# Transposing the expert activations: a scratch round trip and VectorE block turns in place of TensorE transposes

## The chip, the cores and the metric

The program runs on 1 core of a Trainium2 chip. The metric is device time in microseconds (us): the span of the core from its first to its last instruction and what lies around it. Lower is better.

## What is computed

A one-layer decoder trunk on 2048 tokens of width 1024, in float32: LayerNorm, a mixer (a projection, pooling and a gated convolution, an output projection), LayerNorm, and a mixture of experts, LayerNorm. The change touches the last part only, whose core is

```python
# each token goes to 2 of 16 experts; rows are sorted by expert and padded to blocks of 128
def expert_block(args):
    xb, e = args                                   # xb (128, 1024)
    hid = jax.nn.silu(xb @ w1[e]) * (xb @ w3[e])   # w1, w3 (1024, 512)
    return hid @ w2[e]                             # w2 (512, 1024)

ybuf = lax.map(expert_block, (xbuf.reshape(n_blocks, EXPERT_BLOCK, d), blk_e))
```

## The kernel before

**Three products for one.** Every float32 operand is split into a high part (`_hi`, a cast to float32r on ScalarE) and the rest (`_lo`, a subtraction on VectorE). `three` (lines 520 to 522) makes a product of three matmuls: high by high, low by high, high by low.

**Blocks and turns.** In these inputs there are 40 blocks, numbered 0 to 39. TensorE (PE in the profile) goes through one turn for each. In turn b it computes `xb @ w1` of block b (24 matmuls, `up(e_of, 0)`), `xb @ w3` (24, `up(e_of, 1)`), transposes the gathered rows of block b+1 (`x_tile`, 8 transposes of 128x128, line 560), computes `hid @ w2` of block b-1 (24, `down`), and transposes the activations of block b (`hid_tile(b)`, 4 transposes into the PSUM bank `aux`, line 830). The blocks 0, 1 and 39 are partly written out by hand; blocks 2 to 38 are a loop.

**The other engines in turn b**, each in the order of its program:

- ScalarE (ACT): four words of the block table (`value_load`), `hid_hi(b-1)` (copies `aux` to `ht_hi`, line 1106), `silu(b)` after the first 24 matmuls (line 1113), if block b is its expert's last the casts of the next expert's two `w1` units (line 921, 1.9 us each), `final_scale`, `gate_col`, `x_hi(b+1)`, if b is an expert's last the two casts of `w3`, and, after `down` has ended and if block b-1 was its expert's last, the two casts of `w2`.
- VectorE (DVE): three table words, `hid_lo(b-1)` (`ht_lo`, line 1586), the two subtractions of `w1` units if b is an expert's last (line 1649, 2.2 us each), `hid_rows(b)` (`hid`, line 1580), `x_lo(b+1)` (`xt_lo`, line 1570), the two subtractions of `w3`, then, after `down(b-1)`, `final_sums` and `final_rows` of block b-1, and the two subtractions of `w2` if block b-1 was its expert's last.
- GpSimd (POOL): index copies, the gather of `xg` for a later block (line 1953), the put and the gather of running sums, `orow` (line 1929, one add over 128x1024), the store of finished rows.
- SyncE issues the 1 MB loads of weight units, one expert ahead, each when the subtraction of the same unit of the expert before is done.

Units of a weight lie in one place only (`ring_hi`, `ring_lo`), so the next expert's `w1` is split between the end of the first 24 matmuls of an expert's last block and the start of the next turn. This text calls a turn in which block b is its expert's last a **switch turn**. Where an expert has two blocks, the turn ahead of its switch turn is the one after the last switch, and the split of its own `w2` ends in the switch turn itself: a **two-block switch turn**. There are six of these, and eight **three-block switch turns**, which have a turn more in between.

Of the kernel before, what the change touches and what calls it, by code (L numbers as in the profile page):

```python
# [29 lines left out]
ALU = mybir.AluOpType  # L30
# [33 lines left out]
ROW = D + NE  # L64
ALIGN = 128
# [29 lines left out]
def build(nc, x, ln_in_g, ln_in_b, w_in, pool_w, pool_scale, conv_w, conv_b, w_out, ln1_g, ln1_b,  # L95
# [15 lines left out]
    w2_v = exp_w2[0].rearrange("(g i) (k p) n -> i g p k n", p=P, g=NEG)  # L111

    with ExitStack() as ctx:
# [174 lines left out]
        hid = e("hid", [P, DE])  # L288
        ht_hi = e("ht_hi", [P, FT, P], F32R)
# [132 lines left out]
        s_htr = sem("hid_transposed")  # L422
        s_hthi = sem("hid_t_hi")
# [34 lines left out]
        def _(sp):  # L458
# [32 lines left out]
            def load_expert(ex, j):  # L491
                v = (w1_v, w3_v, w2_v)[j // 2]
                kts = v.shape[3] // 2
                src = v[ex // NEG, ex % NEG, :, (j % 2) * kts:(j % 2 + 1) * kts, :]
                dst = staged(j)[:, 0, :].rearrange("p (k c) -> p k c", k=kts)
                sp.dma_start(dst, src).then_inc(s_stage[j], 16)
# [20 lines left out]
        def _(pe):  # L517
# [359 lines left out]
            pe.wait_ge(s_plist, 1)  # L877
            hid_tile(1)
# [5 lines left out]
            with pe.Fori(2, nb1) as b:  # L884
# [11 lines left out]
                hid_tile(b)  # L896
# [16 lines left out]
        def _(act):  # L913
# [4 lines left out]
            def split_hi_expert(ex, j):  # L918

                act.wait_ge(s_stage[j], (ex + 1) * 16 + (MU // 2 * 32 if j < 2 else 0))  # L920
                nc.scalar.copy(ring_hi[:, j:j + 1, :], staged(j)).then_inc(s_ehi[j // 2], 1)  # L921
# [180 lines left out]

            def hid_hi(b):
                act.wait_ge(s_htr, b + 1)
                bank = hid_0[:] if isinstance(b, int) and b == 0 else aux[:].rearrange("p (k t) -> p k t", t=P)
                nc.scalar.copy(ht_hi[:], bank).then_inc(s_hthi, 1)
# [20 lines left out]
            def turn(b, first):  # L1127

                e_of = act.value_load(table[0:1, 0, bass.ds(b, 1)], min_val=0, max_val=NE - 1)
                e_next = act.value_load(table[0:1, 0, bass.ds(b + 1, 1)], min_val=0, max_val=NE - 1)  # L1130
                ends = act.value_load(table[0:1, 1, bass.ds(b, 1)], min_val=0, max_val=1)
# [27 lines left out]
            for t in range(TPC):  # L1159
                act.wait_ge(s_ahout[t], 16 * NCH)  # L1160
            silu(0)
# [10 lines left out]
            ended = act.value_load(table[0:1, 1, bass.ds(nb1 - 1, 1)], min_val=0, max_val=1)  # L1172
            hid_hi(nb1 - 1)
            silu(nb1)
            nb2 = act.value_load(nblocks[0:1, 2:3], min_val=NE - 1, max_val=NB - 2)
            final_scale(nb2)
            act.wait_ge(s_htr, nb)
# [9 lines left out]
        def _(dve):  # L1187
# [197 lines left out]
            def route_hots(c, last=False):  # L1385
# [19 lines left out]
                for k in range(2):  # L1405
                    if last and k == 1:
# [4 lines left out]
                        hid_rows(0)  # L1411
# [161 lines left out]
            def hid_rows(b):  # L1573
                dve.wait_ge(s_silu, b + 1)
                dve.wait_ge(s_w3, b + 1)
                if not (isinstance(b, int) and b == 0):
                    dve.wait_ge(s_htr, b)
                dve.wait_ge(s_gcol, b + 1)
                col = gate_0 if isinstance(b, int) and b == 0 else gate[:, bass.ds(b, 1)]
                V.scalar_tensor_tensor(out=hid[:], in0=act_a[:], scalar=col, in1=acc[1][:], op0=ALU.mult,  # L1580
                                       op1=ALU.mult).then_inc(s_hid, 1)
# [50 lines left out]
            ch.mark(V.tensor_copy(table[:, 1, :], f_next[:]))  # L1632
# [81 lines left out]
            def turn(b, first, split=True):  # L1714
                e_of = dve.value_load(table[0:1, 0, bass.ds(b, 1)], min_val=0, max_val=NE - 1)
                ends = dve.value_load(table[0:1, 1, bass.ds(b, 1)], min_val=0, max_val=1)
# [13 lines left out]
                if first:  # L1730
                    hid_lo(b)
# [316 lines left out]
```

## Time and profile before

| | us |
|---|---|
| median of 3 runs | 1350.07 (1349.74 to 1353.28) |
| span of the profiled execution | 1348.3 |
| its first 634 us | mixer and routing, untouched by the change |
| turns of blocks 2 to 39 | from about 651 to 1328 |
| PE busy | 1311.4 (97% of the span) |
| DVE, ACT, POOL busy | 958.4, 511.7, 525.1 |

Only the span of the profiled execution is known, not a time of its own; the median lies 1.8 us above it. Times of rows are counted from the start of the span. A matmul of 128x512 is listed with some 390 ns, but a new one starts every 0.227 us, since they overlap.

### The profile page before, as it was taken

To read this page: it belongs to the slowest core of one execution; us is meant where nothing else is said; L and a number is where in the kernel's file an instruction comes from. 1 tells how busy PE (TensorE), PEld (TensorE's weight loads), DVE (VectorE), ACT (ScalarE), POOL (GpSimd) and SP (SyncE) were. 2 spreads that over 40 slices of the span, in tenths; PEclk is the share of its full clock that TensorE was granted. 3 is DMA by queue.
4 is the path that set the end of the run, shared out by engine and by line. 5 is a ranking of instruction groups with operands and counts; after the bars stand their busy time and mean duration, and the time that the engine had idled before them with its cause. 6 is when DMAs were issued, how large, how long until landed. Compare 5 with 4: busy or idle time off the path is not lost. (4 is left out here: it accounts for less than half of the span.)

```text
span 1348.3 us, 20368 instructions
## 1 busy us (share of the span) xinstructions
PE 1311.4 (97%) x6382; PEld 1095.8 (81%) x6383; DVE 958.4 (71%) x1357; ACT 511.7 (38%) x568; POOL 525.1 (39%) x543
## 2 busy tenths in 40 slices
PE   5999999999999999998999999999999999999995
PEld 5888888888888888887888888888888888888884
DVE  7758577687759785698777886665675677776564
ACT  3423234322443234323444454343443454434241
POOL 2001010111101110022566665755665656666555
PEclk9999999999999999999999999999999999999998
DMA  9625434563455344544777774563554545666421
GB/s 266 181 89 162 149 111 163 170 192 109 156 186 158 110 141 159 208 181 169 287 263 256 271 270 147 193 234 132 181 202 181 191 164 214 236 231 238 142 69 64
DMA packets 156522, 243.58 MB, mean 181 GB/s; under 512 B 18944, under 2 KB 84992, under 8 KB 156480
## 3 DMA queue, kind: packets, MB, share of 16 engines
q1 hardware_dynamic: 118624, 154.15, 35.3%
q0 software_dynamic: 28928, 71.74, 15.0%
q10 hardware_dynamic: 8928, 17.13, 3.7%
q8 instruction: 26, 0.43, 0.1%
q14 instruction: 16, 0.13, 0.0%
HBM read 211.97 MB, written 64.62 MB: 205 GB/s over the span
## 5 line engine op out<-in xcount | busy, mean ns | idle before, releaser
L520 PE MATMUL acc<-ring_hi 128*128 128x512 f32 (+1 forms) x800 | 308.8, 386 | 2.1 <-DVE ring_lo L1239 1.9
L522 PE MATMUL acc<-ring_hi,ring_lo 128*128 128x512 f32 (+1 forms) x800 | 305.6, 382 | 0.0
L521 PE MATMUL acc<-ring_lo,ring_hi 128*128 128x512 f32 (+1 forms) x800 | 305.3, 382 | 0.0
L520 PE MATMUL acc<-ring_hi,xt_hi 128*128 128x512 f32 x648 | 256.7, 396 | 4.1 <-issue 2.8
L522 PE MATMUL acc<-ring_hi,xt_lo 128*128 128x512 f32 x648 | 252.8, 390 | 0.0
L521 PE MATMUL acc<-ring_lo,xt_hi 128*128 128x512 f32 x648 | 252.4, 390 | 0.0
L1802 POOL TENSOR_TENSOR small<-small 128x1 f32<-128x1 f32 x31 | 47.4, 1527 | 360.8 <-DVE small L1208 360.8
L520 PEld LDWEIGHTS acc<-ring_hi 128*128 128x128 f32 x800 | 151.3, 189 | 30.1 <-DVE ring_lo L1239 2.5
L522 PEld LDWEIGHTS acc<-ring_hi,ring_lo 128*128 128x128 f32 x800 | 151.2, 189 | 29.1
L521 PEld LDWEIGHTS acc<-ring_lo,ring_hi 128*128 128x128 f32 x800 | 151.3, 189 | 27.7
L921 ACT CAST ring_hi<-stage_x 128x2048 fp32r<-128x2048 f32 x64 | 119.4, 1915 | 76.3 <-PE acc L522 75.8
L520 PEld LDWEIGHTS acc<-ring_hi,xt_hi 128*128 128x128 f32 x648 | 121.8, 188 | 30.3 <-issue 5.9
L522 PEld LDWEIGHTS acc<-ring_hi,xt_lo 128*128 128x128 f32 x648 | 121.6, 188 | 25.8
L521 PEld LDWEIGHTS acc<-ring_lo,xt_hi 128*128 128x128 f32 x648 | 121.8, 188 | 23.9
L1649 DVE TENSOR_TENSOR ring_lo<-stage_x,ring_hi 128x2048 fp32r<-128x2048 f32 x60 | 136.7, 2318 | 0.2
L916 ACT CAST ring_hi<-stage 128x2048 fp32r<-128x2048 f32 x47 | 89.7, 1908 | 103.5 <-PE acc L522 97.3
L1929 POOL TENSOR_TENSOR orow<-arow,b 128x1024 f32<-128x1024 f32 x39 | 106.5, 2731 | 48.6 <-ACT arow L1120 48.6
L520 PE MATMUL acc<-ring_hi,ht_hi 128*128 128x512 f32 x312 | 125.3, 401 | 0.0
L1194 DVE TENSOR_TENSOR ring_lo<-stage,ring_hi 128x2048 fp32r<-128x2048 f32 x47 | 107.6, 2289 | 21.1 <-ACT ring_hi L916 21.0
L522 PE MATMUL acc<-ring_hi,ht_lo 128*128 128x512 f32 x312 | 122.0, 391 | 0.0
L521 PE MATMUL acc<-ring_lo,ht_hi 128*128 128x512 f32 x312 | 121.5, 389 | 0.0
L1661 DVE TENSOR_TENSOR rrow<-srow,acc 128x512 f32<-128x512 f32 x78 | 49.9, 680 | 95.1 <-PE acc L522 95.1
(276 smaller groups left out, 1884.0 us busy)
## 6 DMA issues: line engine op xcount, KB each, us to landing
stage_x<-in_exp_w SPq DMA_DIRECT2D x64, 1024.0 KB, 6.2
stage<-in_w_in SPq DMA_DIRECT2D x64, 512.0 KB, 5.4
stage<-in_exp_w SPq DMA_DIRECT2D x32, 1024.0 KB, 6.6
stage<-in_w_out SPq DMA_DIRECT2D x32, 512.0 KB, 5.3
h_scratch<-hres POOLq DMA_DIRECT2D x16, 512.0 KB, 3.0
sum_scratch<-hres ACTq DMA_DIRECT2D x16, 512.0 KB, 2.9
hrow<-in_x POOLq DMA_DIRECT2D x12, 512.0 KB, 4.8
h_scratch<-hrow POOLq DMA_DIRECT2D x12, 512.0 KB, 3.0
```

The lines of the kernel that those rows point to most:

```text
L520: nc.tensor.matmul(dst, w_hi, x_hi, start=start, stop=False)
L521: nc.tensor.matmul(dst, w_hi, x_lo, start=False, stop=False)
L522: return nc.tensor.matmul(dst, w_lo, x_hi, start=False, stop=stop)
L916: nc.scalar.copy(ring_hi[:, slot:slot + 1, :], staged(slot_in)).then_inc(s_hi, 1)
L921: nc.scalar.copy(ring_hi[:, j:j + 1, :], staged(j)).then_inc(s_ehi[j // 2], 1)
L1194: V.tensor_tensor(lo, staged(slot_in), hi.bitcast(F32), ALU.subtract).then_inc(s_lo, 1)
L1649: V.tensor_tensor(ring_lo[:, j:j + 1, :], staged(j), ring_hi[:, j:j + 1, :].bitcast(F32), ALU.subtract).then_inc(s_elo[w], 1)
L1661: ins = V.tensor_tensor(rrow[:, cols], srow[:, cols], acc[2 + n][:], ALU.add)
L1802: G.tensor_tensor(rstd[:], vareps[:], half[:], ALU.pow).then_inc(s_rstd, 1)
L1929: G.tensor_tensor(orow[:], arow[:], b_2[:], ALU.add).then_inc(s_fo, 1)
```

## The change

The activations of a block no longer go through TensorE. ScalarE stores `hid` (256 KB) in a scratch tensor in HBM, and reads it back with four DMAs of 64 KB, one for each group of 32 partitions, so that partition group a holds columns 128a to 128a+127 of all rows (`hid_q`). One VectorE instruction then transposes all 32x32 blocks of `hid_q` into `aux`. The rows of `w2` are loaded in the matching order, with four DMAs a unit in place of one. Blocks 0 and 39 still use the TensorE transposes; there `hid_rows` writes its columns in that order with four instructions in place of one. The high and low parts of `ht` follow as before, though on ScalarE `silu(b)` now comes ahead of `hid_hi(b-1)`. Row 1 of the block table holds one packed word a block (expert, is it the last of its expert, was the block before), so ScalarE and VectorE read one word a turn.

```diff
-    w2_v = exp_w2[0].rearrange("(g i) (k p) n -> i g p k n", p=P, g=NEG)
+    w2_v = exp_w2[0].rearrange("(g i) (a k c) n -> i g a c k n", a=QUARTERS, c=SUB, g=NEG)
+    hid_dram = nc.dram_tensor("hid_scratch", (P, DE), F32).ap()
+    hid_quarters = hid_dram.rearrange("(b r) (a f) -> a r b f", r=SUB, a=QUARTERS)
...
+                    for a in range(QUARTERS):
+                        src = w2_v[ex // NEG, ex % NEG, a, :, (j % 2) * 2:(j % 2 + 1) * 2, :]
+                        dst = staged(j)[a * SUB:(a + 1) * SUB, 0, :].rearrange("p (k c) -> p k c", k=2)
+                        sp.dma_start(dst, src).then_inc(s_stage[j], 16)
...
                 down(pe_of)
-                hid_tile(b)
...
+            def hid_out(b):
+                act.wait_ge(s_hid, b + 1)
+                act.wait_ge(s_hq, b * 16 * QUARTERS)
+                act.dma_start(hid_dram, hid[:]).then_inc(s_hst, 16)
+
+            def hid_back(b):
+                act.wait_ge(s_hst, b * 16 + 16)
+                for a in range(QUARTERS):
+                    act.dma_start(hid_q[a * SUB:(a + 1) * SUB, :].rearrange("r (b f) -> r b f", f=P), hid_quarters[a])\
+                        .then_inc(s_hq, 16)
...
+                word = act.value_load(table[0:1, 1, bass.ds(b, 1)], min_val=0, max_val=4 * NE - 1)
...
                 if not first:
-                    ended = act.value_load(table[0:1, 1, bass.ds(b - 1, 1)], min_val=0, max_val=1)
+                    silu(b)
                     hid_hi(b - 1)
-                    silu(b)
...
                 x_hi(b + 1)
+                hid_out(b)
                 with act.If(ends > 0):
...
                     units_hi(e_of + 1, 1)
+                hid_back(b)
...
+            def hid_turn(b):
+                dve.wait_ge(s_hq, b * 16 * QUARTERS)
+                V.transpose(aux[:].rearrange("p (k b c) -> p k b c", k=FT, c=SUB),
+                            hid_q[:].rearrange("p (b k c) -> p k b c", k=FT, c=SUB)).then_inc(s_hturn, 1)
...
+                word = dve.value_load(table[0:1, 1, bass.ds(b, 1)], min_val=0, max_val=4 * NE - 1)
...
                 if not first:
-                    ended = dve.value_load(table[0:1, 1, bass.ds(b - 1, 1)], min_val=0, max_val=1)
-                    if split:
-                        hid_lo(b - 1)
+                    hid_turn(b)
+                    hid_lo(b - 1)
```

How the order of the instructions moves is seen best at two places. On ScalarE, in the loop over the blocks, from the copy of `aux` to the casts of `w1` (`ring_hi<-stage`), before:

```order
L1133 TENSOR_LOAD table_221
L1133 ISA x2
L1106 CAST ht_hi_209<-aux 128x512 [waits hid_transposed]
L1113 ACTIVATE act_a_207<-acc0 128x512 [waits hid_rows,w1_used]
L1136 COMPARE_AND_BRANCH
L920 ISA
L921 CAST ring_hi<-stage 128x2048 [waits stage0_in]
L921 CAST ring_hi<-stage 128x2048 [waits stage1_in]
```

The same place in the changed kernel (`hid_quarters_turned` is raised by the new VectorE instruction):

```order
L1157 TENSOR_LOAD table_222
L1157 ISA x2
L1137 REGISTER_ALU
L1141 ACTIVATE act_a_207<-acc0 128x512 [waits hid_rows,w1_used]
L1134 CAST ht_hi_210<-aux 128x512 [waits hid_quarters_turned]
L1163 REGISTER_ALU
L1163 COMPARE_AND_BRANCH
L932 ISA
L933 CAST ring_hi<-stage 128x2048 [waits stage0_in]
L933 CAST ring_hi<-stage 128x2048 [waits stage1_in]
```

The copy to `ht_hi` now stands between the silu and the casts of `w1`, and waits for VectorE. On VectorE, from the end of one turn (the `w2` subtractions) to the `w1` subtractions of the next, in the changed kernel:

```order
L1699 TENSOR_TENSOR ring_lo<-stage_x_226,ring_hi 128x2048 [waits w2_hi]
L1782 UNCONDITIONAL_BRANCH
...
L1627 STREAM_TRANSPOSE aux<-hid_q_209 128x512 [waits hid_quarters_in]
L1633 TENSOR_TENSOR ht_lo_211<-aux,ht_hi_210 128x512 [waits hid_t_hi]
L1771 REGISTER_ALU
L1771 COMPARE_AND_BRANCH
L1698 ISA
L1699 TENSOR_TENSOR ring_lo<-stage,ring_hi 128x2048 [waits w1_hi]
```

Before, `ht_lo` followed the `w2` subtractions with nothing between; now the block transpose of `hid_q` comes first, and `ht_lo` needs the ScalarE copy of what it wrote. Later in the turn, ScalarE has the store of `hid` (waits `hid_rows`) between `x_hi` and the casts of `w3`, which before followed each other:

```order
L1109 CAST xt_hi_205<-tp1 128x512 [waits x_transposed]
L1118 ISA [waits hid_rows]
L1119 DMA hid_scratch<-hid_208 128x512 [waits hid_quarters_in]
L1177 COMPARE_AND_BRANCH
L932 ISA
L933 CAST ring_hi<-stage_x_226 128x2048 [waits stage2_in]
```

So the casts of `w3` have come to stand behind the VectorE instruction that writes `hid`.

## Rows read from the trace of the kernel before

**Rows 1.** The page: busy time of the engines and their shares of the span.

```profile
PE 1311.4 (97%) x6382; PEld 1095.8 (81%) x6383; DVE 958.4 (71%) x1357; ACT 511.7 (38%) x568; POOL 525.1 (39%) x543
```

**Rows 2.** Waits of PE: who waited for whom, total us, times, longest.

```profile
PE acc L520 <- DVE xt_lo L1570: 1.3, 4, 0.4
```

**Rows 3.** PE in order of time: start us, us, what [idle before].

```profile
722.75 0.49 PE L520 MATMUL acc<-ring_hi,xt_hi 128*128 128x512 f32 x1 [0.19 <-issue]
...
911.99 1.04 PE L560 MATMUL tp<-ident,xg 128*128 128x128 f32 x8
912.92 0.49 PE L520 MATMUL acc<-ring_hi,ht_hi 128*128 128x512 f32 x1
...
918.01 0.39 PE L521 MATMUL acc<-ring_lo,ht_hi 128*128 128x512 f32 x1
918.24 0.40 PE L522 MATMUL acc<-ring_hi,ht_lo 128*128 128x512 f32 x1
...
918.83 0.48 PE L520 MATMUL acc<-ring_hi,xt_hi 128*128 128x512 f32 x1
919.15 0.39 PE L521 MATMUL acc<-ring_lo,xt_hi 128*128 128x512 f32 x1
```

**Rows 4.** The tile hid: the PE transposes of it, their count and durations.

```profile
L830 PE MATMUL aux<-ident,hid x156: 270/272/273, 649.4 to 1323.3; 128*128 128x128 f32 x156
```

**Rows 5.** ScalarE in order of time, in a two-block switch turn.

```profile
710.35 0.60 ACT L1113 ACTIVATE act_a<-acc 128x512 f32<-128x512 f32 x1 [1.51 <-PE acc L522]
710.84 3.71 ACT L921 CAST ring_hi<-stage 128x2048 fp32r<-128x2048 f32 x2
```

**Rows 6.** VectorE in order of time, in the same turn.

```profile
708.89 4.49 DVE L1649 TENSOR_TENSOR ring_lo<-stage_x,ring_hi 128x2048 fp32r<-128x2048 f32 x2
713.30 0.68 DVE L1586 TENSOR_TENSOR ht_lo<-aux,ht_hi 128x512 fp32r<-128x512 f32 x1
713.90 6.69 DVE L1649 TENSOR_TENSOR ring_lo<-stage,ring_hi 128x2048 fp32r<-128x2048 f32 x2
...
721.17 1.28 DVE L1570 TENSOR_TENSOR xt_lo<-tp,xt_hi 128x512 fp32r<-128x512 f32 x2
```

**Rows 7.** GpSimd in order of time, in the same turn and the next.

```profile
715.69 2.75 POOL L1929 TENSOR_TENSOR orow<-arow,b 128x1024 f32<-128x1024 f32 x1 [2.27 <-ACT arow L1120]
...
722.92 2.65 POOL L1953 DMA_INDIRECT xg<-h_scratch,gat_now  x1 [0.87 <-POOL gat_now L1943]
```

**Rows 8.** ScalarE: silus of three turns, and two copies that wait for the gather.

```profile
889.01 0.60 ACT L1113 ACTIVATE act_a<-acc 128x512 f32<-128x512 f32 x1 [2.42 <-PE acc L522]
...
911.91 0.19 ACT L1101 COPY gate<-xg  x1 [3.34 <-DMA xg<-h_scratch,gat_now]
...
924.59 0.60 ACT L1113 ACTIVATE act_a<-acc 128x512 f32<-128x512 f32 x1 [1.49 <-PE acc L522]
...
942.28 0.60 ACT L1113 ACTIVATE act_a<-acc 128x512 f32<-128x512 f32 x1 [2.42 <-PE acc L522]
...
1123.28 0.19 ACT L1101 COPY gate<-xg  x1 [2.18 <-DMA xg<-h_scratch,gat_now]
```

**Rows 9.** VectorE in the three-block switch turn of the silu at 889.01.

```profile
891.44 4.49 DVE L1649 TENSOR_TENSOR ring_lo<-stage,ring_hi 128x2048 fp32r<-128x2048 f32 x2 [1.41 <-ACT ring_hi L921]
...
897.82 4.75 DVE L1649 TENSOR_TENSOR ring_lo<-stage_x,ring_hi 128x2048 fp32r<-128x2048 f32 x2
```

**Rows 10.** GpSimd: the gather of rows issued after that turn.

```profile
903.86 1.04 POOL L1953 DMA_INDIRECT xg<-h_scratch,gat_now  x1 [0.89 <-DVE rrow L1661]
```

**Rows 11.** DMA issues: what, queue, count, KB each, median us from issue to landing.

```profile
sum_scratch<-hres ACTq DMA_DIRECT2D x16, 512.0 KB, 2.9
...
xg<-h_scratch,gat_now POOLq DMA_INDIRECT x39, 4.4
...
h1t<-in_pool_w ACTq DMA_DIRECT2D x1, 256.0 KB, 6.6
```

**Rows 12.** ScalarE in order of time: what a DMA issue takes of its sequencer.

```profile
614.57 0.33 ACTq L975 DMA_DIRECT2D sum_scratch<-hres  x1
```

More of the change, by code:

```diff
@@ L288, in build @@
         hid = e("hid", [P, DE])
+        hid_q = e("hid_q", [P, DE])
         ht_hi = e("ht_hi", [P, FT, P], F32R)
@@ L1571, in x_lo, with hid_rows @@
                                     ALU.subtract).then_inc(s_xtlo, 1)
-            def hid_rows(b):
+            def hid_rows(b, by_tile=False):
                 dve.wait_ge(s_silu, b + 1)
                 dve.wait_ge(s_w3, b + 1)
-                if not (isinstance(b, int) and b == 0):
-                    dve.wait_ge(s_htr, b)
+                if isinstance(b, int) and b == 1:
+                    dve.wait_ge(s_htr, 1)
+                elif not (isinstance(b, int) and b == 0):
+                    dve.wait_ge(s_hst, b * 16)
                 dve.wait_ge(s_gcol, b + 1)
                 col = gate_0 if isinstance(b, int) and b == 0 else gate[:, bass.ds(b, 1)]
-                V.scalar_tensor_tensor(out=hid[:], in0=act_a[:], scalar=col, in1=acc[1][:], op0=ALU.mult,
-                                       op1=ALU.mult).then_inc(s_hid, 1)
+                if by_tile:
+                    tiles = hid[:].rearrange("p (k a c) -> p a k c", k=FT, c=SUB)
+                    parts = [(tiles[:, a], *(t[:, a * P:(a + 1) * P].rearrange("p (k c) -> p k c", c=SUB)
+                                             for t in (act_a, acc[1]))) for a in range(QUARTERS)]
+                else:
+                    parts = [(hid[:], act_a[:], acc[1][:])]
+                for to, x_a, x_b in parts:
+                    ins = V.scalar_tensor_tensor(out=to, in0=x_a, scalar=col, in1=x_b, op0=ALU.mult, op1=ALU.mult)
+                ins.then_inc(s_hid, 1)
+            def hid_turn(b):
+                dve.wait_ge(s_hq, b * 16 * QUARTERS)
+                V.transpose(aux[:].rearrange("p (k b c) -> p k b c", k=FT, c=SUB),
+                            hid_q[:].rearrange("p (b k c) -> p k b c", k=FT, c=SUB)).then_inc(s_hturn, 1)
             def hid_lo(b):
@@ L1712, in final_last, with turn @@
                                        op0=ALU.mult, op1=ALU.add).then_inc(s_fo, 1)
-            def turn(b, first, split=True):
-                e_of = dve.value_load(table[0:1, 0, bass.ds(b, 1)], min_val=0, max_val=NE - 1)
-                ends = dve.value_load(table[0:1, 1, bass.ds(b, 1)], min_val=0, max_val=1)
+            def turn(b, first):
+                word = dve.value_load(table[0:1, 1, bass.ds(b, 1)], min_val=0, max_val=4 * NE - 1)
+                e_of, ends, ended = (word >> 2).with_bounds(min_val=0, max_val=NE - 1), word & 2, word & 1
                 if not first:
-                    ended = dve.value_load(table[0:1, 1, bass.ds(b - 1, 1)], min_val=0, max_val=1)
-                    if split:
-                        hid_lo(b - 1)
+                    hid_turn(b)
+                    hid_lo(b - 1)
                 with dve.If(ends > 0):
@@ L1738, in turn_last @@
             def turn_last(b, prev):
[L1739 removed]
+                ended = dve.value_load(table[0:1, 1, bass.ds(b, 1)], min_val=0, max_val=4 * NE - 1) & 1
+                hid_turn(b)
                 hid_lo(b - 1)
[L1741 removed]
+                hid_rows(b, True)
                 dve.wait_ge(s_hthi, b + 1)
@@ L1750, in _ @@
             dve.wait_ge(s_elo[2], 2)
+            dve.sem_inc(s_hturn, 1)
             turn(1, True)
             nb1 = dve.value_load(nblocks[0:1, 1:2], min_val=NE, max_val=NB - 1)
-            turn(2, False, split=False)
-            with dve.Fori(3, nb1) as b:
+            with dve.Fori(2, nb1) as b:
                 turn(b, False)
```

49 lines of the change are left out of this document (28 added, 21 removed).

## The prediction, made before the changed kernel ran

> **What bounds the kernel now.** First the page: PE is busy 97% of the span, every other engine 71% or less [rows 1]. Then the waits of PE: in all the turns it loses only 1.3 us to VectorE's `xt_lo`, in four waits [rows 2]. So the time is the sum of what PE issues, and taking work off PE is worth its full price, as long as nobody else comes late. Then the timelines of one turn, engine by engine, since the question is who has little room. A turn is counted here from PE's first matmul of it; its silu stands 5.76 us in (918.83 [rows 3], 924.59 [rows 8]). An undisturbed turn lasts 942.28 - 924.59 = 17.69 us [rows 8]. A two-block switch turn lasts longer: silu at 710.35 [rows 5], so it begins at 704.59, and the next begins at 722.75 [rows 3]: 18.16 us, since `xt_lo` comes late. VectorE has no room in these turns.
>
> **The transposes taken off PE.** Two matmuls in a row start 0.23 us apart (918.01, 918.24), but from 918.24 to the second matmul after the four transposes, 919.15, it is 0.91 us [rows 3]: they cost 0.91 - 2 x 0.23 = 0.45 us. There are 156 / 4 = 39 such groups [rows 4], and the one of block 39 stays: 38 x 0.45 = **17.3 us less**. An undisturbed turn becomes 17.24 us. The low bound of the gain is what the loop's branch might take by itself once no short transposes stand there: a 0.19 us gap was seen at a turn's start [rows 3], which would leave 10 us of the 17.
>
> **The table words.** ScalarE's and VectorE's table reads stand where these engines wait for PE anyway (ScalarE's silu waits for PE in every turn) or run under the subtractions ahead of them. I cost them at nothing. Not below nothing either: PE would gain only if it waited for them, and it waits 1.3 us in all [rows 2].
>
> **The round trip through scratch.** No row shows this store and this load. The nearest: a 512 KB store of ScalarE lands after 2.9 us, a 256 KB load of 512 B pieces after 6.6 us [rows 11], and an issue takes ScalarE 0.33 us [rows 12]. So from `hid` to `hid_q` it takes 2.9 + 4 x 0.33 + 4.4 to 6.6 = 9 to 11 us. `hid` is written some 12 us into the turn (VectorE's `hid_rows` waits for PE's 48 matmuls), so it is back at 21 to 23, that is 4 to 6 us into the next turn. `ht_lo` is needed when `down` starts, 912.92 against a start at 900.95: 12.0 us in [rows 3, 8]. In undisturbed turns the round trip is hidden, and I cost it at nothing. The DMA page of the Trainium skill (DMA: Bandwidth & Descriptors, the rule on batching) says that transfers under 64 KB are descriptor-dominated; four of 64 KB lie at that edge, and it would matter only if the cover were gone.
>
> **The VectorE transpose** is not in the trace either. Its nearest row is `ht_lo`, 0.6 us from start to start for 128x512 (713.30 to 713.90 [rows 6]); the upper bound is one pass of four times the size, 2.2 us [rows 9]. I take 0.6.
>
> **Two-block switch turns.** Here the added chain is in the open. Before, ScalarE cast `w1` from 710.84 [rows 5], 6.25 us in, long ahead of VectorE. Now these casts stand behind the copy to `ht_hi`, that behind the block transpose, and that behind the two `w2` subtractions. Step by step, us into the turn: the `w2` subtractions began at 708.89 - 704.59 = 4.3 [rows 6], now at 4.7, as the turn begins sooner after `down` ends; two take 4.4, to 9.1; block transpose 0.6, to 9.7; copy 0.6, to 10.3; first cast 1.9 (half of 3.71 [rows 5]), to 12.2; two `w1` subtractions 4.4, to 16.6; `hid` 0.65 and the first `xt_lo` 0.6, to 17.85; PE starts the next turn 0.98 us after the second `xt_lo` begins (721.77 to 722.75 [rows 3, 6]): 18.8 us. That is 1.6 us over 17.24, where before it was 0.47 over 17.69: 1.1 more, six times: **6.7 us more**. One delay disappears in this: before, the two `w1` subtractions took 6.69 instead of 4.4 us [rows 6], because `orow` (from 715.69 [rows 7]) held the second one up. With `arow` 4 us later, `orow` comes to start at 15.1, when the second subtraction (14.4 to 16.6) is already running.
>
> **The gather of the next rows.** `x_tile` needs `xg`, and POOL issues that gather behind `orow` and the subtractions of `w3`. In the trace: `w3` subtractions from 897.82 to 902.5 [rows 9], gather at 903.86 [rows 10], data there at 911.91 (ScalarE waited for it [rows 8]), `x_tile` at 911.99 [rows 3], just in time. Another such turn had it at 1123.28, 1.2 us earlier in the turn [rows 8]. So the slack is 0.1 to 1.2 us.
> Three-block switch turn, changed: the casts of `w3` now wait for `hid` and a DMA issue, and `hid` comes 0.5 later since `ht_hi` is copied ahead of the `w1` casts. The first `w3` subtraction, before 897.82 - 883.25 = 14.6 us in, moves to about 16.2, its pair ends at 20.6, the gather goes out at 22.0, which is 4.8 us into the next turn where it was 2.9. 1.9 later, less the slack, is 0.7 to 1.8 us of waiting of PE; none if POOL's short copies slip in between the two subtractions. I take 0.8, eight times: **6.4 us more**.
> After a two-block switch turn: `orow` ends at 16.6 + 2.4 = 19.0; gather 4.5 us behind its end as before (718.4 to 722.92 [rows 7]) or 5.6 as in the other turn, so 4.7 to 5.8 us into the next turn, and later still if it waits for the `w3` subtractions, which end 5.4 into it. With a landing of 4.4 (the median [rows 11]) to 8.0 us (903.86 to 911.9) it is there between 9.1 and 14, needed at 11.0: 0 to 3 us. `ht_lo` alone costs 0.3 there (start 11.2, usable 12.1, wanted 11.9). I take 1.7, six times: **10.2 us more**.
> The Trainium skill (SBUF — State Buffer, "Who interferes with whom") says that a VectorE instruction with two SBUF inputs and a GpSimd instruction that reads SBUF exclude each other, first come first served. The trace agrees: 6.69 us for the pair of subtractions beside `orow`.
>
> **Start and end.** Two added table instructions and two times four `hid_rows` pieces in place of one: **0.8 us more**.
>
> **The sum.** 1350.07 - 17.3 + 6.7 + 6.4 + 10.2 + 0.8 = **1356.9 us**; on the profiled execution 1348.3 + 6.8 = 1355.1 of span. The differences are taken from that execution and put on the median, 1.8 us above its span. What a measurement of this kernel can tell from no change is 0.3%, 4 us: under 1346.0 is faster, over 1354.1 slower.
>
> **Rivals.**
> 1. *The gathers keep their time*: POOL's copies slip between the subtractions and `xg` lands in 4.4 us. Then only `ht_lo`'s 0.3 x 6 and the switch turns are left: 1350.07 - 17.3 + 6.7 + 1.8 + 0.8 = 1342 us, faster. For it: median landing. Against: 8 us in the very turn in question, beside two 1 MB weight loads.
> 2. *VectorE becomes the bound*, slower: a block transpose of 1.3 us instead of 0.6. Each 0.7 goes straight into the six two-block switch turns and the six after them, and in the turns behind a three-block switch's `w2` split `ht_lo` slips past 12.0: 0.7 x 12 + 0.2 x 8 = 10 more, 1367 us. It decides from 0.9 us on.
> 3. *`orow` gets in first* in the two-block switch turn: the second `w1` subtraction waits 2.2 us, six times, 13 more: 1370 us. The page named above gives the pair to whichever starts first; here the two are 0.7 us apart.
> 4. *The freed time isn't freed*: the loop's end costs 0.19 us a turn by itself: 7 more, 1364 us.
> 5. *The round trip is late*, over 15 us: PE waits in every turn, 1380 us or more. The scratch rows of the page speak against it.
>
> **How the numbers follow.** Forecast 0.37 (from 1349 to 1362, by the two gathers' bounds), rival 1 0.31 (1336 to 1348), rival 2 0.12, rival 3 0.06, rival 4 0.08, rival 5 0.06. The range 1338 to 1374 leaves out rival 5, the end of rival 3 and 0.04 at the low end. Faster: most of rival 1, 0.28. Same: its upper end and the forecast's lower part, 0.24. Slower: the rest, 0.48.
>
> **What would show each step.** PE: two matmuls across a turn's start 0.23 us apart; undisturbed turns of 17.24 us. In the two-block switch turns: `w1` casts near 10.3 us in, length near 18.8. PE's waits: a new one of `x_tile` for `xg`, 6 and 8 times, some 0.8 to 1.7 us each; if it is missing, rival 1 holds. `STREAM_TRANSPOSE` near 0.6 us. The forecast is wrong if these turns come out at 17.3 to 17.7 us.

## The result, and the profile after

| | us |
|---|---|
| before, median of 4 runs | 1350.2 (1349.74 to 1353.28) |
| changed, median of 4 runs | 1449.78 (1445.17 to 1455.29) |
| ratio | 1.0734, 95% interval 1.0716 to 1.0753 |
| span of the profiled execution | 1448.3 (before: 1348.3) |
| forecast | 1356.9, range 1338 to 1374 |

The change costs 7.3%. The forecast was 93 us too low, and the time lies outside its range. The head of the page after, first the engines (it answers to [rows 1]), then the DMA queues with packets, MB and their share of 16 engines' span, then issues with KB each and the median us from issue to landing:

```profile
PE 1337.0 (92%) x6230; PEld 1107.5 (76%) x6231; DVE 973.1 (67%) x1402; ACT 510.2 (35%) x568; POOL 538.8 (37%) x543
...
q10 hardware_dynamic: 36288, 37.06, 7.9%
...
stage<-in_exp_w SPq DMA_DIRECT2D x32, 1024.0 KB, 7.5
...
stage_x<-in_exp_w SPq DMA_DIRECT2D x32, 1024.0 KB, 9.4
```

152 transposes fewer, and still PE is busy 26 us longer (1311.4 before). ScalarE's queue moves 20 MB more in 27,000 more packets. PE now waits (who waited for whom, total us, times, longest; it answers to [rows 2], where all of `xt_lo` was 1.3 us):

```profile
PE tp L575 <- DMA xg<-h_scratch,gat_now: 53.2, 13, 4.5
PE acc L535 <- DVE ht_lo L1633: 16.1, 8, 9.9
...
PE acc L535 <- DVE xt_lo L1601: 8.3, 7, 1.4
```

**Where the time went.** I measured the length of each turn in the traces, from PE's first matmul of it to the next one's. The 37 turns of the loop took 658.6 us before and 759.1 after: the difference, 100.5, is all of the loss. By kind of turn, means in us:

| turns | before | forecast | after |
|---|---|---|---|
| 8 undisturbed ones | 17.70 | 17.24 | 17.22 |
| 8 three-block switch turns | 17.70 | 17.24 | 17.23 |
| 6 two-block switch turns | 18.26 | 18.8 | 18.74 |
| 6 behind a two-block switch turn | 17.72 | 18.9 | 24.10 |
| 7 behind a three-block switch turn | 17.72 | 18.0 | 25.42 |
| block 38, behind the last switch | 17.69 | 18.0 | 17.25 |
| block 2, the loop's first | 17.74 | 17.2 | 31.23 |

So 22 turns came out to a few hundredths as forecast, and 13 turns behind a switch, and block 2, hold all of the loss that was missed. Block 2 stands behind a switch as well, that of block 1, which is partly written out by hand; the forecast had no term for it, and the 17.2 in the table is only the undisturbed turn. The turn of block 38 is behind a switch too, but no expert is left to load, and it takes 17.25 us, less than forecast: a first hint.

**One such turn.** It is that of block 16, from 948.30 to 972.60. SyncE's and ScalarE's issues ahead of it (start us, us of the issuing engine, what, how many):

```profile
943.72 2.59 SPq L505 DMA_DIRECT2D stage<-in_exp_w  x2
951.50 2.57 SPq L505 DMA_DIRECT2D stage_x<-in_exp_w  x2
...
946.66 0.35 ACTq L1119 DMA_DIRECT2D hid_scratch<-hid  x1
...
953.28 2.17 ACTq L1125 DMA_DIRECT2D hid_q<-hid_scratch  x4
956.79 0.60 ACT L1141 ACTIVATE act_a<-acc 128x512 f32<-128x512 f32 x1 [5.83 <-issue]
```

The store of `hid` goes out behind the two 1 MB loads of `w1`. ScalarE can issue the loads of the quarters when it has landed, 6.6 us later, and by then the two loads of `w3` are ahead of them. VectorE, GpSimd and PE, with the idle time before each and what ended it:

```profile
963.40 0.73 DVE L1627 STREAM_TRANSPOSE aux<-hid_q 128x512 f32<-128x512 f32 x1 [5.34 <-DMA hid_q<-hid_scratch]
964.78 0.69 DVE L1633 TENSOR_TENSOR ht_lo<-aux,ht_hi 128x512 fp32r<-128x512 f32 x1 [0.65 <-ACT ht_hi L1134]
...
954.97 1.04 POOL L2001 DMA_INDIRECT xg<-h_scratch,gat_now  x1 [0.89 <-DVE rrow L1711]
...
963.66 1.97 PE L575 MATMUL tp<-ident,xg 128*128 128x128 f32 x8 [4.30 <-DMA xg<-h_scratch,gat_now]
965.61 0.79 PE L535 MATMUL acc<-ring_hi,ht_hi 128*128 128x512 f32 x1
966.20 0.63 PE L536 MATMUL acc<-ring_lo,ht_hi 128*128 128x512 f32 x1
```

The quarters are in at 963.40, that is 16.7 us after the store was issued (14.4 to 18.3 us in the 13 turns of this kind). The forecast had 9 to 11. In undisturbed turns it is some 12.5 us, more than forecast too (from the store to the block transpose, blocks 11 and 12), but there nobody waits for it. The gather is in 8.7 us after its issue. PE waits 4.30 us for it, then `x_tile` takes 1.97 us where it took 1.04 [rows 3], and matmuls start 0.43 us apart instead of 0.23. The same turn in pieces (us, busy time of the engines, granted clock, DMA share, GB/s):

```profile
948.30:955.00 6.70, 6.70 (x31) 5.54 (x30) 5.69 (x4) 2.66 (x2) 4.29 (x6) 1.00 0.90 281
955.00:960.00 5.00, 4.36 (x20) 3.28 (x18) 2.84 (x5) 0.60 (x1) 4.41 (x5) 1.00 1.04 338
960.00:965.00 5.00, 1.34 (x7) 1.35 (x8) 0.95 (x2) 0.84 (x2) 0.00 (x0) 0.69 0.69 253
965.00:970.00 5.00, 5.00 (x16) 3.75 (x16) 2.47 (x4) 1.85 (x4) 3.22 (x2) 0.63 0.20 71
```

The DMA engines are full until 960 (a share of 0.90, then 1.04), and the granted clock falls to 0.69 and 0.63 once PE has stood still. These are means over both levels of it, as PE's own rows show:

```profile
967.90 0.63 PE L537 MATMUL acc<-ring_hi,ht_lo 128*128 128x512 f32 x1
968.33 0.57 PE L535 MATMUL acc<-ring_hi,ht_hi 128*128 128x512 f32 x1
...
968.97 0.39 PE L537 MATMUL acc<-ring_hi,ht_lo 128*128 128x512 f32 x1
969.20 0.40 PE L535 MATMUL acc<-ring_hi,ht_hi 128*128 128x512 f32 x1
```

Until 968.3 matmuls start 0.43 us apart (1.2 GHz), behind it 0.23 (2.4 GHz). PE is busy 20.0 us in this turn for work that takes 17.2 in others. Two things are late by nearly the same amount, the gather (15.4 us into the turn, needed at 10.9) and the quarters (15.1, so that `down` can start at some 17). This trace alone doesn't say which of them costs, or whether the landings or the places of the issues are to blame.

### The profile page after: what moved, and what is told of

The parts are those of the page before. It is cut to its first block and busy times, and to the rows that moved or that the text cites. A ratio compares the mean times of both kernels' runs of the same rounds, so it can differ in the third digit from the quotient of the medians.

```text
span 1448.3 us, 19960 instructions
## 1 busy us (share of the span) xinstructions
PE 1337.0 (92%) x6230; PEld 1107.5 (76%) x6231; DVE 973.1 (67%) x1402; ACT 510.2 (35%) x568; POOL 538.8 (37%) x543
## 3 DMA queue, kind: packets, MB, share of 16 engines
q0 software_dynamic: 28928, 71.74, 14.4%
## 5 line engine op out<-in xcount | busy, mean ns | idle before, releaser
L535 PE MATMUL acc<-ring_hi,xt_hi 128*128 128x512 f32 x648 | 253.8, 392 | 10.2 <-DVE xt_lo L1601 8.3
L1977 POOL TENSOR_TENSOR orow<-arow,b 128x1024 f32<-128x1024 f32 x39 | 113.3, 2905 | 190.6 <-ACT arow L1148 190.6
L535 PE MATMUL acc<-ring_hi,ht_hi 128*128 128x512 f32 x312 | 138.3, 443 | 16.2 <-DVE ht_lo L1633 16.1
L536 PE MATMUL acc<-ring_lo,ht_hi 128*128 128x512 f32 x312 | 132.2, 424 | 0.0
L537 PE MATMUL acc<-ring_hi,ht_lo 128*128 128x512 f32 x312 | 131.4, 421 | 0.0
```

What stands on the lines that cost most here:

```text
L535: nc.tensor.matmul(dst, w_hi, x_hi, start=start, stop=False)
L536: nc.tensor.matmul(dst, w_hi, x_lo, start=False, stop=False)
L537: return nc.tensor.matmul(dst, w_lo, x_hi, start=False, stop=stop)
L1977: G.tensor_tensor(orow[:], arow[:], b_2[:], ALU.add).then_inc(s_fo, 1)
```

## The experiments

Three theories: TRIP, the round trip is late because of the weight loads that stand beside it; GATHER, the gather is issued too late; ORDER, the packed word and ScalarE's new order (silu ahead of `hid_hi`). All times below are medians of 4 or 5 runs with a ratio to before (1350.3 to 1351.6 us on the same chips), save for number 4, a single run.

**1. TensorE transposes again, all else kept.**

```diff
+                hid_tile(b)                 # after down
-                hid_out(b)
-                hid_back(b)
-                    hid_turn(b)
```

> The changed kernel with the TensorE transposes back for every block and without the round trip: what is left of the change is the packed word, silu ahead of the copy to ht_hi, w2 loaded with four DMAs a unit, and hid written with four instructions (1.4 us for 0.75). Theory TRIP (the 100 us come from the round trip through scratch and what it holds up): 1348 to 1356 us, no turn over 19 us. Rival ORDER (silu ahead of ht_hi, or the split w2 loads, cost it): over 1380 us.

Measured: 1355.42, ratio 1.0041 (1.0027 to 1.0055). ORDER falls. Of what is left, some 5 us, most lies in the turns of blocks 2 to 4 (58.6 us where they were 53.9, the longest 20.07, so "no turn over 19 us" missed). The trace shows what changed there. These lines of the change belong to it. The kernel before has VectorE's first blocks written apart, with `ht_lo` ahead of the sums of block 0:

```diff
-                if first:
-                    hid_lo(b)
                 final_sums(b - 1)
...
-            turn(2, False, split=False)
-            with dve.Fori(3, nb1) as b:
+            with dve.Fori(2, nb1) as b:
```

VectorE's `ht_lo` of block 1 in the kernel before, 5.3 us into the turn of block 2:

```profile
655.97 0.68 DVE L1586 TENSOR_TENSOR ht_lo<-aux,ht_hi 128x512 fp32r<-128x512 f32 x1
```

The same in number 1, 12.5 us into the turn, behind sums that wait for a gather:

```profile
660.11 1.28 DVE L1705 TENSOR_TENSOR rrow<-srow,acc 128x512 f32<-128x512 f32 x2 [1.45 <-DMA srow<-sum_scratch,sum_now]
...
664.80 0.69 DVE L1627 TENSOR_TENSOR ht_lo<-aux,ht_hi 128x512 fp32r<-128x512 f32 x1 [0.24 <-issue]
```

PE then waits 1.2 us for it, and 1.1 and 0.8 us for VectorE in the two turns behind. No run puts these lines back by themselves, so this is a reading of the trace and not a test.

**2. No traffic.** VectorE transposes `hid` itself.

```diff
-                            hid_q[:].rearrange("p (b k c) -> p k b c", k=FT, c=SUB))
+                            hid[:].rearrange("p (b k c) -> p k b c", k=FT, c=SUB))
```

> The changed kernel without the store and the four loads; VectorE transposes the 32x32 blocks of hid itself, so rows and columns of different groups are not exchanged, which leaves out the exchange between the groups of 32 partitions. Theory TRIP: the turns after a switch fall from 24 to 18 us, the two-block switch turns stay at 18.7, total 1338 to 1350 us. Rival GATHER (the gather of xg goes out late, behind VectorE's splits and GpSimd's lock, whatever the round trip does): x_tile still starts 14 to 15 us into the turns after a switch, 14 such turns of 21 to 22 us, total over 1385 us.

Measured: 1363.52, ratio 1.0101 (1.0084 to 1.0118). Above TRIP's 1350 and far below GATHER's 1385. The turns behind a switch take 19.90 (two blocks) and 17.79 us (three), against a forecast of 18.9 and 18.0. So the gather terms of the forecast were of the right size, and 86 of the 100 us belong to the round trip, with all that it holds up. Block 2's turn takes 22.46 us even here, 4.7 more than before.

**3. The kernel before, with the store and the four loads added for nothing.**

```diff
+                hid_out(b)                  # after x_hi(b + 1)
+                hid_back(b)                 # after the casts of w3
```

> The kernel before with the same store and four loads added on ScalarE in every turn, their result unused; TensorE transposes as before. It adds the traffic, ScalarE's waits for it and its place ahead of the w3 casts. Theory TRIP by traffic and by ScalarE's waits: gathers land 1 to 2 us later, turns after a switch 19 to 21 us, total 1370 to 1395 us. If only the wait of ht_hi for the landed quarters costs: 1350 to 1356 us.

Measured: 1375.77, ratio 1.0191 (1.0174 to 1.0208). Though nobody reads what comes back, it costs 25 us, again in the turns behind a switch (19.2 and 19.5 instead of 17.7). The others keep their length, save block 2's.

**4. The changed kernel with a quarter of the bytes in the weight loads** of experts 2 to 15 (they then compute with stale weights in places). A single run.

```diff
+                    if ex >= 2:
+                        dst, src = dst[:, 0:1], src[:, 0:1]
```

> The changed kernel with the weight loads of experts 2 to 15 cut to a quarter of the bytes (the rest of each unit keeps old values, so the products are of wrong weights). Theory TRIP by congestion (store, loads and gathers share the DMA engines with 4 MB of weights around a switch): store lands in 3 us in place of 6 to 9, quarters in 5, the gather in 4.5 in place of 8.7; turns after a switch 17.3 to 18.5 us, total 1335 to 1350 us. If the lateness is of issue and not of landing: these turns stay over 21 us, total over 1385 us.

Measured: 1348.62, that is 101 us below the changed kernel, though all instructions of the round trip are there. In its trace, ScalarE in the switch turn that answers to the one above:

```profile
902.81 0.35 ACTq L1123 DMA_DIRECT2D hid_scratch<-hid  x1
905.64 1.76 ACTq L1129 DMA_DIRECT2D hid_q<-hid_scratch  x4
```

And on its page, the median landing of the quarters:

```profile
hid_q<-hid_scratch ACTq DMA_DIRECT2D x152, 64.0 KB, 2.2
```

The store lands in 2.8 us instead of 6.6, the quarters in 2.2. The first was in the forecast (2.9 [rows 11]), the second even below it. The sizes of the forecast are right where the weight loads are small.

**5 to 8. Which wait, and which side to mend.** Four kernels on one chip. In 5, GpSimd issues the gather some 10 us earlier, ahead of `orow`. In 6, SyncE holds the loads of `w1` and `w3` until the late transpose is done. Number 7 is both. In 8, the traffic and ScalarE's waits stay, and VectorE transposes `hid` itself.

```diff
+                    if ex >= 2 and j == 0:      # 6, 7: SyncE, ahead of load_expert
+                        sp.wait_ge(s_clear, ex - 1)
...
+                    with dve.If(ended > 0):     # VectorE, behind hid_lo(b - 1)
+                        dve.sem_inc(s_clear, 1)
```

> The changed kernel, but GpSimd issues the gather of the next rows some 6 to 10 us earlier, ahead of its add of orow and of its waits for VectorE. In the turn after a switch both xg (landed 15.3 us in) and the quarters of hid (15.1 us in) came late, so the two can't be told apart there. TRIP (the round trip through scratch is late by itself, beside the weight loads): x_tile is back at 10.9 us, but the product of the activations still starts some 16 to 17.3 us in; only the wait's place moves and the time stays at 1425 to 1445 us. GATHER (the late gather of rows is what costs, and what it delays delays the rest): the turns after a switch fall to 18 or 19 us and the time to 1355 to 1375 us.

> The changed kernel, but SyncE holds the 1 MB loads of w1 and w3 of an expert until VectorE has transposed the activations of the last block of the expert two before it, one semaphore more; all bytes are still moved. TRIP (queued behind weight loads): the store lands again in some 3 us and the quarters in 4 to 7, the product of the activations starts at 12.0 to 12.6 us in the turns after a switch, these take 17.5 to 20 us (the gather of rows is still issued 6.6 us in, now beside the held loads), and the time is 1350 to 1385 us. Rival COVER (the loads have no slack to give away): the casts of w1 of the two-block experts wait for their loads, every two-block switch turn grows by more than 4 us, and the time stays above 1400 us. Rival OWN (the trip is slow by itself, the weight loads have no part): 1435 us or more.

> Both edits of the two runs above together. TRIP: neither the gather nor the round trip meets the weight loads, the turns after a switch come down to 17.2 to 18.5 us, the two-block switch turns stay at 18.8, and the time is 1335 to 1355 us. GATHER: the same as with the early gather alone. COVER: above 1395 us.

> The changed kernel with its store and its four loads in every turn, but VectorE transposes hid itself and not what came back (the exchange between the groups of 32 partitions is left out of the result); so all traffic and all of ScalarE's waits are there, and only VectorE's wait for the quarters is gone. It measured 1363.5 us without the traffic, and the traffic alone cost 25 us in the kernel before. TRIP: 1380 to 1400 us, the rest of the 86 us being VectorE's wait for the quarters itself. If the traffic and ScalarE's waits alone do it (they delay the gather and the casts, and nobody needs the quarters late): 1425 us or more.

Measured: 5, 1458.66, ratio 1.0804 (1.0786 to 1.0822); 6, 1419.21, 1.0519 (1.0495 to 1.0542); 7, 1426.24, 1.0570 (1.0548 to 1.0591); 8, 1413.11, 1.0460 (1.0435 to 1.0486).

With the early gather PE's wait for `xg` is gone and comes back in full one step later:

```profile
PE acc L535 <- DVE ht_lo L1633: 81.7, 15, 7.7
```

So mending the gather alone gains nothing: its 53.2 us of waits stood in front of the round trip's. The time is even 9 us above the changed kernel's, and above TRIP's 1445.

Number 6 did what TRIP said where it was aimed: the turns behind a switch take 18.00 and 17.46 us. But its time missed TRIP's 1385. The wait had moved one turn on:

```profile
708.50 0.94 SPq L506 DMA_DIRECT2D stage<-in_exp_w  x2
709.48 2.87 SPq L506 DMA_DIRECT2D stage_x<-in_exp_w  x2
...
710.00 0.35 ACTq L1122 DMA_DIRECT2D hid_scratch<-hid  x1
718.57 1.76 ACTq L1128 DMA_DIRECT2D hid_q<-hid_scratch  x4
...
730.60 0.73 DVE L1630 STREAM_TRANSPOSE aux<-hid_q 128x512 f32<-128x512 f32 x1 [3.45 <-DMA hid_q<-hid_scratch]
...
732.80 0.79 PE L538 MATMUL acc<-ring_hi,ht_hi 128*128 128x512 f32 x1 [6.11 <-DVE ht_lo L1636]
```

The held loads, 4 MB at once, now meet the next block's store: 8.6 us to land, 20.6 us until the quarters are in, and these turns take 24 us where they took 18.7 (21.6 instead of 17.2 with three blocks). This shows TRIP's cause better than the expected time would have: the lateness goes where the loads go. COVER isn't it: the casts of `w1` have their data. Number 7, for which TRIP said 1335 to 1355, missed in the same way: its two-block switch turns take 25.2 us, and PE waits 58.8 us for `ht_lo`. Number 8 came out between its two expectations (up to 1400, or 1425 and more); number 12 takes it apart.

**9 to 12. How many loads beside one round trip, and ScalarE's part.** In 9 only `w3` is held (`j == 2` above), in 10 `w1` is held as in 6 while `w3` and `w2` wait for the `w2` subtractions, 11 is 10 with the early gather. In 12, as in 8, nobody reads `hid_q`, and ScalarE doesn't wait for the store either:

```diff
-    hid_quarters = hid_dram.rearrange("(b r) (a f) -> a r b f", r=SUB, a=QUARTERS)
+    hid_quarters = h1_dram[0:P, 0:DE].rearrange("(b r) (a f) -> a r b f", r=SUB, a=QUARTERS)
...
-                act.wait_ge(s_hst, b * 16 + 16)
```

> The changed kernel, but in the turn after a switch SyncE holds the two 1 MB loads of w3 until VectorE has transposed the activations; those of w1 (issued some 15 and 17 us into the switch turn, beside the store) stay. With w1 and w3 both held the late round trip moved one turn on, since the next block's store and quarters then met 4 MB of loads. TRIP (what counts is how many loads stand beside a round trip): the store stays late (landed 5 us in), the quarters come back in 4 to 7 us instead of 9, the product of the activations starts 12 to 14 us in, the turns after a switch take 19 to 21 us, the turn behind them grows by 0 to 2, and the time is 1375 to 1405 us. Rival SUM (only the bytes count, wherever they stand, and the lateness is handed on in full): 1415 us or more.

> The changed kernel with the weight loads spread: w1 waits for the block transpose in the turn after a switch, w3 and w2 wait for the w2 subtractions one turn later. (It relies on every expert having two blocks or more, as in these inputs.) TRIP: no round trip meets more than 2 MB of weight loads, all transposes run 9 to 11 us into their turns, the turns after a switch take 17.3 to 18.8 us, the two-block switch turns 18.8 to 20, and the time is 1350 to 1375 us. Rival SUM: the lateness goes to other turns, 1400 us or more.

> The loads spread as in the run above and the gather of rows issued ahead of orow. With the round trip out of the burst the gather is what is left of the waits in the turns after a switch (0.5 to 1 us each with small loads). TRIP: 5 to 12 us below the run above, 1342 to 1368 us. If the early gather meets the store of hid (issued 12 to 13 us in) and delays it beyond its slack, as with the loads in place, it is as slow as that run or slower.

> The unused round trip again (VectorE transposes hid itself; the exchange between groups of 32 partitions is left out of the result), but the four loads read another tensor of the same pitch, so ScalarE issues them at once and does not wait for the store to land. All traffic is there, ScalarE is never held for a landing. With ScalarE's wait it measured 1413 us, with no traffic 1363.5. If the traffic does it (the gather of rows lands later beside it): 1400 to 1415 us. If ScalarE's wait does it (silu at 8 instead of 5.8 us, everything behind it later): 1365 to 1385 us.

Measured: 9, 1382.97, ratio 1.0224 (1.0202 to 1.0247); 10, 1471.13, 1.0908 (1.0875 to 1.0941); 11, 1473.26, 1.0900 (1.0882 to 1.0918); 12, 1386.43, 1.0255 (1.0238 to 1.0272).

Holding two loads, all bytes still moved, gives back 67 of the 100 us, and SUM (only the bytes count) falls. The turns behind a switch take 18.1 and 17.9 us; what is left lies one turn on, where the next store meets the held `w3` (20.9 us in two-block switch turns, 19.3 in undisturbed ones). The round trip of number 9 that answers to the one above:

```profile
861.43 2.58 SPq L506 DMA_DIRECT2D stage<-in_exp_w  x2
877.39 0.92 SPq L506 DMA_DIRECT2D stage_x<-in_exp_w  x2
...
864.37 0.35 ACTq L1122 DMA_DIRECT2D hid_scratch<-hid  x1
870.30 1.81 ACTq L1128 DMA_DIRECT2D hid_q<-hid_scratch  x4
...
875.75 0.73 DVE L1630 STREAM_TRANSPOSE aux<-hid_q 128x512 f32<-128x512 f32 x1
```

The store still takes 5.9 us beside `w1`. The quarters, with no `w3` ahead of them, are in before VectorE has ended its subtractions: the transpose has no idle time before it. Numbers 10 and 11 missed by 100 us. I had laid `w3` and `w2` where I thought that no round trip stood, but these 4 MB go out 11.7 to 16.5 us into a turn whose store goes out at 14.6, and the turn behind that takes 25.8 us. It is the same fault as in number 6, and mine: I had placed loads by when they are needed, not by which store is due.

Numbers 2, 12, 8 and the changed kernel are a ladder, each with one thing more:

| | us | step | PE's waits for `xg`, us |
|---|---|---|---|
| no round trip (2) | 1363.5 | | 13.2 |
| its traffic (12) | 1386.4 | 23 | 29.5 |
| and ScalarE waits for the store (8) | 1413.1 | 27 | 44.7 |
| and VectorE waits for the quarters (changed) | 1449.8 | 37 | 53.2 |

So 50 of the 86 us come about though nobody needs what the round trip brings: its traffic and ScalarE's wait make the gather of the next rows late. Number 12 landed just above the 1385 us that its expectation gave to ScalarE's wait, and it shows both parts. The step of 27 is not of the wait alone: in number 12 the quarters also go out beside the store and not behind it.

ScalarE's part had no place in the forecast. From its store's landing on depends when it gets to the silu: in the turn of block 16, 8.5 us in instead of 5.6.

**13 to 15. The clock, and the blocks that meet no loads.** Numbers 13 and 15 add 8 and 16 useless matmuls to each turn, number 14 sends only blocks through scratch that are not their expert's last.

```diff
+                for _ in range(8):          # ahead of x_tile(b + 1)
+                    nc.tensor.matmul(tp[0][:], xt_hi[:, 0, :], xt_hi[:, 0:4, :], start=True, stop=True)
```

```diff
+                with pe.If(ends > 0):       # 14, after down
+                    hid_tile(b)
...
+                with act.If(ends < 1):
+                    hid_out(b)
+                    hid_back(b)
...
+                    with dve.If(ended < 1):
+                        hid_turn(b)
```

> The changed kernel with 8 more matmuls of 128x512 in every turn, into the bank that the transposes of x overwrite right behind them: 8 x 0.227 = 1.8 us of useless work of PE in each of 37 turns, 67 us in all. CLOCK (PE's idle time of over 4 us in the turns after a switch also halves its clock for the work behind it, some 3 us a turn): the waits shrink by more than 1.8 us since the switch turn ends later too and PE keeps its clock; undisturbed turns 19.0 us, turns after a switch 20.5 to 22.5 us where they were 22.8 to 26.7, granted clock 0.98 or more, time 1425 to 1450 us, no slower than without the added work. If the clock has no part: every turn grows by up to 1.8 us save for what the waits absorb, turns after a switch 23 to 26 us, 1470 to 1495 us.

> The same with 16 matmuls, 3.6 us a turn, 134 us of added work in all. CLOCK: the late round trip and the gather fit into the longer turns, all turns take 20.8 to 21.5 us save the first two, granted clock 0.99, time 1460 to 1480 us (37 turns of 20.84 us are 771 us, where the changed kernel took 759 us for them). Without a part of the clock, and with the landings as late as before: 1500 us or more.

> Only the blocks that are not their expert's last go through scratch and the VectorE block transpose; the last block of an expert, whose round trip would meet the loads of w1 and w3, is transposed by TensorE as before (columns written in the matching order). TRIP (a round trip outside the burst is hidden): 23 undisturbed turns of 17.21 us or so, three-block switch turns 17.7, two-block switch turns 18.8, turns after a switch 17.3 to 19 by the gather, no wait for the quarters; time 1343 to 1360 us. If a round trip costs by itself wherever it stands, or the branches on TensorE cost 0.2 us a turn: 1362 us or more.

Measured: 13, 1434.85, ratio 1.0626 (1.0608 to 1.0644); 15, 1471.17, 1.0892 (1.0874 to 1.0910); 14, 1377.15, 1.0196 (1.0176 to 1.0216).

Number 13 does 67 us more work on PE and is 15 us faster than the changed kernel. Its page (PE was busy 1337.0 us in the changed kernel):

```profile
PE 1370.7 (96%) x6526; PEld 1141.1 (80%) x6527; DVE 973.6 (68%) x1402; ACT 510.4 (36%) x568; POOL 537.5 (38%) x543
```

PE is busy 33.7 us longer than in the changed kernel, for 67 us more of matmuls: the other 33 are what the low clock had cost (mean granted clock 0.988 against 0.961). The larger part of the gain is not of the clock: PE's idle time falls from 111 to 58 us, since the added work covers waits. Number 15, whose clock is 0.993, has PE busy for 1431.0 us, less 134 of added work, 40 below the changed kernel. In number 13 the turn of block 16, here whole, has the full clock (0.69 and 0.63 in parts of it in the changed kernel):

```profile
940.88:960.33 19.45, 19.30 (x90) 15.87 (x89) 10.02 (x14) 3.29 (x6) 11.50 (x16) 1.00 0.67 232
```

Number 15, with turns of 20.84 to 20.87 us save for block 2 (27.49) and block 8 (21.16), shows that 3.6 us more of room a turn is enough for nearly every round trip. Neither is of use as a kernel.

Number 14 missed its 1343 to 1360. The part on the round trip held: undisturbed turns of 17.21 us, and PE waits for `ht_lo` 4.2 us in all. But the turns behind a switch take 19.1 us, most of what is over 17.2 by the gather, and the two-block switch turns 19.3 to 19.4 (block 3: 21.0), where 18.8 was expected; why these are longer stays open. PE's waits, and one gather with its `x_tile`:

```profile
PE tp L575 <- DMA xg<-h_scratch,gat_now: 18.1, 13, 1.8
```

```profile
864.77 1.04 POOL L2014 DMA_INDIRECT xg<-h_scratch,gat_now  x1 [0.87 <-DVE rrow L1720]
...
872.47 1.09 PE L575 MATMUL tp<-ident,xg 128*128 128x128 f32 x8 [1.81 <-DMA xg<-h_scratch,gat_now]
```

It goes out 5.2 us into the turn instead of 2.9 [rows 10] and takes 7.7 us. ScalarE, held by the store of the block before, comes to the silu at 6.5 us in the switch turn, and `hid`, the casts of `w3` and the gather follow. No complete version here beats the kernel before; number 4, level with it, leaves out most of the weights.

## Why the prediction was wrong, by its own steps

**The transposes taken off PE** were right: 17.22 us for an undisturbed turn, forecast 17.24 (38 x 0.45 is 17.1 and not 17.3, which changes nothing), with the pitch of 0.23 us kept across a turn's start; so rival 4 falls.

```profile
930.85 0.39 PE L537 MATMUL acc<-ring_hi,ht_lo 128*128 128x512 f32 x1
931.08 0.39 PE L535 MATMUL acc<-ring_hi,xt_hi 128*128 128x512 f32 x1
```

**The VectorE transpose** was right: 0.73 us, forecast 0.6, so rival 2 falls.

**The two-block switch turns** were right: 18.74 us, forecast 18.8, and rival 3 falls with them (`orow` starts 15.2 us in, the second `w1` subtraction at 14.5; forecast 15.1 and 14.4).

**The table words** were right as far as the runs tell: all that is left of the change without the round trip and the VectorE transpose is 5 us in three turns (number 1). **Start and end**, 0.8 us, was too low by some 4. That block 1's `ht_lo` moved behind the sums of block 0 had no term at all, and the sum left out block 2 among the turns behind a switch. It took 31.23 us instead of 17.74, so 13.5 of the 100 us, of which 4.7 stay without the round trip (number 2).

**The gather of the next rows** had the right mechanism. With no traffic beside it (number 2) its two terms of 1.7 and 0.8 us were 2.7 and 0.6, so rival 1 falls. In the changed kernel it went out at 6.6 us instead of 4.8, and landed in 8.7 instead of 8.0 at most.

**The round trip through scratch** is the step that failed: "in undisturbed turns the round trip is hidden, and I cost it at nothing." The sentence is true of undisturbed turns. The sum used it for all turns. In the turns behind a switch the round trip is back after 14.4 to 18.3 us where the sum had 9 to 11, the cause is the loads of the weights (numbers 4, 6 and 9), and with what it holds up it costs 86 us (number 2) where the sum had nothing. Three faults led there.

First, the landings were medians of a store in the mixer's part and a load of its start [rows 11], while the question was of a stretch with 4 MB of weight loads in it. The row that I should have read is the one of the kernel before in a two-block switch turn (last two numbers: DMA share, GB/s):

```profile
704.60:722.75 18.15, 17.96 (x88) 14.72 (x85) 17.82 (x16) 14.23 (x12) 12.84 (x11) 1.00 0.72 249
```

The DMA engines were 72% busy on the mean of that turn, and a mean hides the burst: in stretches of 5 us their share is 0.53 up to 715, and 0.96 to 1.02 from there to 735. The first of these:

```profile
715.00:720.00 5.00, 5.00 (x28) 4.21 (x27) 5.00 (x2) 4.45 (x6) 3.40 (x2) 1.00 1.02 408
```

The gather's 8.0 us "in the very turn in question" stood in the prediction, as an argument against rival 1, and was not applied to the round trip, which has two landings in a row at the same place. Rival 5 named this outcome, with 1380 us or more and a chance of 0.06 (it had PE wait in every turn, which it did not), and the argument against it was the row with the wrong neighbours.

Second, who waits behind a wait: `hid_back` holds ScalarE until the store has landed, and the silu of the next turn stands behind it. This was up to 27 of the 86 us (number 8 less number 12). The prediction named what is queued behind the waits for VectorE, not what stands behind ScalarE's wait for the landing.

Third, a wait of PE was priced at its length. After 4.3 us of it PE ran at 1.2 GHz for the next 4.7 us, 2.8 us of busy time more in that turn, and 33 to 40 us in all by numbers 13 and 15.

The size of the pieces had no great part: in number 4 the 64 KB loads land in 2.2 us. What the Trainium skill says of transfers under 64 KB (DMA: Bandwidth & Descriptors, the rule on batching), cited in the prediction for the case that the cover were gone, did not decide it.

## What to carry to other kernels

A round trip through memory is priced with landings taken beside the loads that will stand beside it, so the DMA share is read first, in stretches as short as the transfer: here a turn's mean of 0.72 had the engines full for its last 8 us and beyond. An engine that issues a transfer on another's completion stands still for it, so price what is queued behind that wait on the issuing engine too. When a late chain is mended, look for the next one of the same length (the gather and the quarters were 0.3 us apart here), and when loads are moved out of one transfer's way, ask whose way they come into.

## What the runs showed of the hardware

- A 256 KB store landed in 2.8 us beside weight loads of 256 KB (number 4), in 5.6 to 7.6 us beside two loads of 1 MB (changed kernel and number 9) and in 8.6 us beside four (number 6), issued around it on another queue. The four loads of 64 KB behind it took 2.2 us (median, number 4), and were in 8.1 to 11.1 us after their issue beside the loads of `w3` (changed kernel).
- The VectorE transpose of 128x512 in 32x32 blocks, SBUF to PSUM in float32: 0.717 to 0.729 us, 38 times.
- The length of a wait alone doesn't tell whether PE's clock falls. After 4.30 us of it `x_tile` took 1.97 us, and full speed came back 4.7 us later (changed kernel, block 16). In number 12 PE stood 3.00 us in block 4 and went on at full clock, but after 1.87 us in block 16 `x_tile` took 1.61 us, and the matmuls behind it started 0.43 us apart until 940.0. The rows of these two:

```profile
705.90 1.09 PE L575 MATMUL tp<-ident,xg 128*128 128x128 f32 x8 [3.00 <-DMA xg<-h_scratch,gat_now]
...
936.50 1.61 PE L575 MATMUL tp<-ident,xg 128*128 128x128 f32 x8 [1.87 <-DMA xg<-h_scratch,gat_now]
```

- Useless matmuls made the changed kernel 15 us faster, 8 in each turn (number 13).
